# Softmax sums of the dilated attention combined as one number a token, and its value products in plain f32

## The chip, the cores and the metric

The kernel runs as one program on 1 core of one Trainium2 chip. A core has TensorE (PE in the profile, its weight loads are PEld), VectorE (DVE), ScalarE (ACT), GpSimd (POOL) and SyncE (SP), which here only issues DMAs. The metric is device time in microseconds (us), the median of some runs; lower is better.

## The reference

The reference is a decoder trunk of two layers over 1024 tokens of width 1024, all in f32. Layer 0 mixes with latent attention (`mla`) and forgetting attention (`fox`); layer 1 mixes with dilated attention and with sparse attention (compressed `cmp`, selected `sel`, window `win`). Each layer ends with an MLP and a gated embedding. What the change touches is the dilated attention: three groups with distances 1, 4 and 16 between keys, four heads each, whose outputs are merged head by head with the softmax denominators as weights:

```
for g, (w, d) in enumerate(((128, 1), (512, 4), (2048, 16))):
    idx = t[:, None] - offsets[g][None, :]                  # keys t, t-d, t-2d, ..
    logits = einsum(q[g], k[g][idx]) * scale + bias
    lse = logsumexp(logits);  p = exp(logits - lse)
    outs.append(einsum(p, v[g][idx]));  lses.append(lse)
wts = softmax(stack(lses, axis=0), axis=0)                  # over the three groups
return einsum('gbhq,gbqhd->bqhd', wts, stack(outs))
```

So each token has, for each head, three minima, three sums and three weights; each weight multiplies 64 output elements.

## The kernel before

All products that must be exact to f32 are made of float32r operands (TensorE's fast format for 4-byte numbers): an operand is split into a high part and the low rest, and two or three products are added up. A projection streams the weights in units (`RAW`, 512 KB a load), POOL makes `WH` (the high part) and `WL` (the rest) of each (lines 873 and 875), and PE multiplies (line 1035).

The attention of a layer is a list of jobs. A job is one kind and one pair of heads; layer 1 has d1, d4, d16, cmp for pair 0, the same four for pair 1, then sel, win, sel, win. `d1`, `d4`, `d16` are the three distances. A job has 16 tasks: 8 blocks of 128 queries for head e=0, then 8 for head e=1. Two tasks are a chunk, four a half. `build_attention` makes a list of steps, one for a task, and every engine walks the same list in order, each doing its part and waiting on semaphores:

- PE: `logits(t)` (line 1181), then `values` of a chunk that ended 5 steps ago (line 1211), then `turn(t)` of the task two steps back, which transposes the probabilities into one of two `TR` banks (line 1195). At the start of a job `turn_v` transposes the values `RV` into the same two banks (line 1159).
- DVE: scale, bias and row minimum of the logits, into `PBS` and `NML` (line 1785). ACT: exponential and row sum (line 1453).
- ACT copies the transposed probabilities from `TR` to `PT` as the high part (line 1447), and DVE subtracts it from `TR` for the low part (line 1796). The values go the same way into `VS` (lines 1436 and 1767). The products of the high part of one head and of the low part of the other fall on the rows of the other head in the bank `OP`, so ACT copies those rows to `CORR` (line 1421) and DVE adds both.
- Dilated only: DVE adds into `DU` (line 1826). When a half of e=1 ends, POOL spreads the row sums and row minima of both heads over 64 columns each (`SPREAD`, line 941, twice), PE transposes them through the same two `TR` banks (`turn_spread`, line 1224, 8 transposes), ACT copies the sums to `DL` (line 1427) and DVE the minima to `DM` (line 1830). `DL` and `DM` so hold each number 64 times, and have the shape of the outputs.
- `merge`: over the steps after d16, that is inside cmp, DVE takes minima, differences, products, sums and reciprocals of 128x1024 tiles (lines 1853 to 1869), ACT exponentials (line 1459), and POOL weights and adds the outputs (lines 950 to 962).

SP issues the loads of the attention in one queue, in order: per job `RV` (512 KB) and for each head six pieces of `QK` (256 KB each) and a `BIAS`. The buffers of `QK` are one for each e, so a load for the next job waits for the last logits of the same e (`s_qk`), line 707. A cmp job needs no `RV` and only two pieces of `QK` a head.

After the attention, POOL makes `WH` and `WL` of the first unit of the output projection once its last `XL` is written.

Of the kernel before, what the change touches and what calls it, by code (L numbers as in the profile page):

```python
# [21 lines left out]
P = 128  # L22
# [63 lines left out]
MERGE_STEPS = 12  # L86
POOL_STEPS = 7
# [102 lines left out]
MERGE_PIECES = 14  # L190
# [22 lines left out]
class Group:  # L213
# [3 lines left out]
    def __init__(self, seq, first, n, tr, half=None, what=None):  # L217
        self.seq, self.ring, self.first, self.n, self.tr = seq, (seq - 1) % 2, first, n, tr
        self.half, self.what = half, what


class Task:


    def __init__(self, no, job, e, i):
# [4 lines left out]
        self.col = no % 16  # L230
# [34 lines left out]
def build_attention():  # L265
# [3 lines left out]
    n = dict(load=0, bias=[0, 0], head=[0, 0], raw=0, ops=0, mask=0, rl=0, spread=0, dl=0, fin=0, xl=0, cor=0, xo=0)  # L269
    phases = {}  # L270
    for name, plan in (("even", EVEN_JOBS), ("odd", ODD_JOBS)):
        ph = Phase()
        ph.name, ph.jobs, ph.tasks = name, [], []
        for kind, pair in plan:
# [6 lines left out]
            for e in range(2):  # L281
# [15 lines left out]
                for h in range(2):  # L297
# [35 lines left out]
    count = dict(seq=0, a=0)  # L333
    groups = []

    def group(first, size, half=None, what=None):
        count["seq"] += 1
        count["a"] += half is None
        groups.append(Group(count["seq"], first, size, count["a"], half, what))
        return groups[-1]  # L340

    for ph in phases.values():
# [3 lines left out]
        merging, ph.merged = [], {}  # L346
        for s in range(len(ts) + VALUE_LAG + 2 + MERGE_PIECES):
# [10 lines left out]
            st.merge = [(p, s - s0) for p, s0 in merging if 0 < s - s0 <= MERGE_PIECES]  # L358
            if st.out and st.out is st.out.job.halves[-1] and st.out.job.kind == "d16":
                merging.append((st.out.job.pair, s))  # L360
                ph.merged[st.out.job.pair] = st.out.fin
# [6 lines left out]
            if st.start and st.start.kind != "cmp":  # L368
                st.start.vgroups = [group(g, 4) for g in range(2)]
            if st.turn:  # L370
                for g0 in range(0, len(st.turn.blocks), 4):
                    st.turn.groups.append(group(g0, min(4, len(st.turn.blocks) - g0)))
                st.turn.turned = count["a"]
            if st.norm and st.norm.e == 1:
                st.norm.groups = [group(0, 4, st.norm, what)
                                  for what in (("sums", "minima") if st.norm.job.kind in DILATED else ("inverse",))]
# [5 lines left out]
    for ph in phases.values():  # L382
        end = Phase()
        end.tasks, end.chunks, end.halves = ph.tasks[-1].no + 1, ph.jobs[-1].chunks[-1].no + 1, ph.jobs[-1].halves[-1].no + 1
# [3 lines left out]
        end.xl, end.fin = ph.jobs[-1].halves[-1].xl, ph.jobs[-1].halves[-1].fin  # L388
# [10 lines left out]
def program(nc, ins, out):  # L399
# [5 lines left out]
    with ctx:  # L405
# [110 lines left out]
        y_h = dram("y_h", (DC, P, S))  # L516
        b_rows = dram("b_rows", (16, BROW_N))
# [57 lines left out]
        s_o = sem("s_o")  # L575
        s_xo = sem("s_xo")
# [6 lines left out]
        s_dl = sem("s_dl")  # L583
# [12 lines left out]
        s_md = sem("s_md")  # L596
        s_cmp = sem("s_cmp")
# [59 lines left out]
        def group_free(eng, g):  # L657

            if g.seq > 2:
                x = pt_groups[g.seq - 3]  # L660
                if x.what == "sums":
                    eng.wait_ge(s_dl, x.half.dl)
                elif x.half:
                    eng.wait_ge(s_fin, x.half.fin)
                else:
                    eng.wait_ge(s_ptD, x.tr)

# [14 lines left out]
        def _(sp):  # L682
# [1505 lines left out]
```

## Time and profile before

| | us |
|---|---|
| median of 3 runs | 3186.12 (3182.68 to 3191.12) |
| profiled execution, its own time | 3180.44 |
| its span (first to last instruction) | 3178.6 |
| PE busy | 2913.9 (92%) |
| DVE busy | 1241.0 (39%) |
| ACT busy | 898.4 (28%) |
| POOL busy | 947.3 (30%) |
| mean granted TensorE clock | 0.961 of full |

The page also cuts the span in 40 equal slices of 79.5 us. In the slices 24 to 27, about 1830 to 2150 us, the busy share of PE falls to 7 to 8 tenths and the one of DVE rises to 4 to 7 tenths; the granted clock there is 0.7 to 0.9. The dilated and compressed jobs of layer 1 lie there. In nearly all other slices PE is at 9 tenths.

A row of the trace's timeline gives start, duration, engine, line of the kernel, operation, written tile<-read tiles, shape and count of merged instructions, and in brackets the idle time before and what ended it. A DMA row shows how long SP took to issue it.

### The profile page before, as it was taken

What the parts mean: (1) busy time and instruction counts of PE and PEld (TensorE: products, weight loads), DVE (VectorE), ACT (ScalarE), POOL (GpSimd) and SP (SyncE); (2) the same over time, 40 slices, a digit from 0 to 9 for tenths busy, and PEclk for the clock granted to TensorE, in tenths of its full rate; (3) what the DMA queues carried; (4) which work ended last, traced back from release to release, by engine and by line L of the source; (5) the groups of instructions that cost most, each with busy time, mean ns of one, the idle gap of its engine ahead of it and who ended that gap; (6) DMA issues with size and microseconds to landing.
All of it is one profiled execution on the core that took longest, in us unless ns stands there. A gap on an engine that the chain in (4) does not pass through costs nothing.

```text
span 3178.6 us, 37130 instructions
## 1 busy us (share of the span) xinstructions
PE 2913.9 (92%) x13684; PEld 2381.1 (75%) x13684; DVE 1241.0 (39%) x1893; ACT 898.4 (28%) x1613; POOL 947.3 (30%) x622
## 2 busy tenths in 40 slices
PE   8996888889999999999999976867889999999999
PEld 5785777767888888876788865756668888888867
DVE  3425777414222222225423147687252222222254
ACT  3304666423110010025200035656340001011141
POOL 2330144342333333342233202121423333333332
PEclk9998999999999999999999986779999999999999
DMA  4336532110111111111235264444201111111111
GB/s 154 126 116 179 126 82 65 74 47 34 47 53 46 46 46 53 46 53 53 80 130 217 80 162 105 113 113 122 80 33 51 49 46 46 51 48 46 60 40 73
DMA packets 73792, 253.67 MB, mean 80 GB/s; under 512 B 9699, under 2 KB 13283, under 8 KB 73367
## 3 DMA queue, kind: packets, MB, share of 16 engines
q1 hardware_dynamic: 58728, 196.35, 20.4%
q10 hardware_dynamic: 14944, 55.74, 4.5%
q8 instruction: 73, 1.20, 0.2%
q14 instruction: 47, 0.39, 0.0%
HBM read 203.99 MB, written 52.78 MB: 81 GB/s over the span
## 4 chain that ended last, share of the span: by engine, by line
PE 80%; DVE 10%; issue 4%; ACT 2%; DMA 2%; POOL 1%; SPq 0%; DVEq 0%; ACTq 0%; POOLq 0%
PE ACC L1035 67%; PE OP L1211 3%; PE ACC L1181 3%; PE TR L1195 3%; PE OP L1105 2%; DVE PT L1796 1%; DVE XL L1653 1%; DVE H L1673 1%; ACT PT L1447 1%; DVE T L1670 1%; PE TR L1224 1%; DVE PB L1785 1%; DVE XF L1842 1%; PE TR L1159 1%; DVE M L1702 0%
## 5 line engine op out<-in xcount | busy, mean ns | idle before, releaser
L873 POOL CAST WH<-RAW 128x1024 fp32r<-128x1024 f32 x203 | 214.2, 1055 | 1544.8 <-PE ACC L1035 1526.2
L1035 PE MATMUL ACC<-XH,WH 128*128 128x512 f32 x1792 | 575.1, 402 | 54.2 <-DVE XL L1653 26.8
L1035 PE MATMUL ACC<-XL,WH 128*128 128x512 f32 x1792 | 557.1, 392 | 0.0
L1035 PE MATMUL ACC<-XH,WL 128*128 128x512 f32 x1792 | 556.5, 392 | 0.0
L875 POOL TENSOR_TENSOR WL<-RAW,WH 128x1024 fp32r<-128x1024 f32 x203 | 491.1, 2419 | 24.8 <-POOL WH L873 1.5
L1035 PEld LDWEIGHTS ACC<-XH,WH 128*128 128x128 f32 x1792 | 338.1, 190 | 153.5 <-issue 72.6
L1035 PEld LDWEIGHTS ACC<-XL,WH 128*128 128x128 f32 x1792 | 339.6, 189 | 71.9
L1035 PEld LDWEIGHTS ACC<-XH,WL 128*128 128x128 f32 x1792 | 339.3, 189 | 71.9
L1409 ACT ACTIVATE HH<-T 128x1024 fp32r<-128x1024 f32 x64 | 67.9, 1061 | 1149.7 <-DVE T L1695 1149.7
L1702 DVE TENSOR_TENSOR M<-M,ACC 128x1024 f32<-128x1024 f32 x128 | 156.3, 1221 | 482.6 <-PE ACC L1035 480.4
L1035 PE MATMUL ACC<-HH,WH 128*128 128x512 f32 x1024 | 316.7, 390 | 3.3 <-DVE M L1702 3.1
L1035 PE MATMUL ACC<-HL,WH 128*128 128x512 f32 x1024 | 315.3, 389 | 0.0
L1035 PE MATMUL ACC<-HH,WL 128*128 128x512 f32 x1024 | 315.2, 389 | 0.0
L1181 PE MATMUL ACC<-QK 128*128 128x512 f32 (+3 forms) x864 | 234.7, 385 | 12.2 <-DMA QK<-y_odds 5.7
L1695 DVE SCALAR_TENSOR_TENSOR T<-ACC,R 128x1024 f32<-128x1024 f32 x64 | 78.4, 1225 | 418.7 <-PE ACC L1035 418.0
L1796 DVE TENSOR_TENSOR PT<-TR,PT 128x512 fp32r<-128x512 f32 (+4 forms) x416 | 191.4, 477 | 108.6 <-ACT PT L1447 104.1
L1035 PEld LDWEIGHTS ACC<-HH,WH 128*128 128x128 f32 x1024 | 191.0, 188 | 48.2 <-issue 9.5
L1035 PEld LDWEIGHTS ACC<-HL,WH 128*128 128x128 f32 x1024 | 192.2, 188 | 40.1
L1035 PEld LDWEIGHTS ACC<-HH,WL 128*128 128x128 f32 x1024 | 192.2, 188 | 40.0
L1447 ACT ACTIVATE PT<-TR 128x512 fp32r<-128x512 f32 (+4 forms) x416 | 168.7, 427 | 171.7 <-PE TR L1195 167.2
L1195 PE MATMUL TR<-IDENT,PB 128*128 128x128 f32 x840 | 135.9, 283 | 54.0 <-DVE PT L1796 21.7
L1181 PEld LDWEIGHTS ACC<-QK 128*128 128x128 f32 x864 | 164.1, 222 | 24.5 <-issue 6.3
(193 smaller groups left out, 3406.0 us busy)
## 6 DMA issues: line engine op xcount, KB each, us to landing
RAW<-in_w SPq DMA_DIRECT2D x203, 512.0 KB, 3.5
QK<-y_odds SPq DMA_DIRECT2D x128, 256.0 KB, 5.1
y_odds<-HALVES ACTq DMA_DIRECT2D x16, 1024.0 KB, 5.3
QK<-y_foxs SPq DMA_DIRECT2D x48, 256.0 KB, 5.5
y_foxs<-HALVES ACTq DMA_DIRECT2D x8, 1024.0 KB, 5.1
y_kv<-Q ACTq DMA_DIRECT2D x8, 512.0 KB, 2.6
BIAS<-y_f SPq DMA_DIRECT2D x8, 512.0 KB, 7.2
H<-in_xT ACTq DMA_DIRECT2D x8, 512.0 KB, 7.2
```

The costliest lines, as they stand in the source:

```text
L873: nc.gpsimd.tensor_copy(WH[:, slot], RAW[:, slot]).then_inc(s_whi, 1)
L875: nc.gpsimd.tensor_tensor(WL[:, slot], RAW[:, slot], WH[:, slot].bitcast(F32), ALU.subtract).then_inc(s_split, 1)
L1035: mm = nc.tensor.matmul(acc[:, h * HALF:(h + 1) * HALF], w(k), x[:, k, h * HALF:(h + 1) * HALF], start=first and k == k0 and w is ws and x ...
L1105: mm = nc.tensor.matmul(OP[:, h], ONES[:], Q[:, (q + c) % 2, h * HALF:(h + 1) * HALF], start=c == 0, stop=c == n - 1)
L1181: mm = nc.tensor.matmul(score_bank(t, c0, c1), x, k[:, c0:c1], start=m == 0, stop=m == len(passes) - 1 and not masked)
L1195: tr = nc.tensor.transpose(TR[0:w, g.ring, y * P:(y + 1) * P], prob(t)[:, x * w:(x + 1) * w], IDENT[:])
L1211: mm = nc.tensor.matmul(OP[:, c.half.no % 2, col + c0:col + c1], v, pt, start=c.opens and n == 0 and hl == 0, stop=c.closes and n == len(o ...
L1409: nc.scalar.activation(HH[:, t.idx], x, ACT.Square).then_inc(s_hhi, 1)
L1447: nc.scalar.activation(PT[0:r, c.buf, 0, k0:k0 + g.n, m * P:(m + 1) * P], src.rearrange("p (k q) -> p k q", q=P), ACT.Copy).then_inc(s_ptA, 1)
L1695: V_.scalar_tensor_tensor(out=x, in0=ACC[:, t.pair], scalar=0.0, in1=R[:], op0=ALU.max, op1=ALU.mult).then_inc(s_evD, 1)
L1702: V_.tensor_tensor(M[:, t.idx], M[:, t.idx], ACC[:, t.pair], ALU.add).then_inc(s_evD, 1)
L1796: V_.tensor_tensor(lo, TR[0:r, g.ring, 0:g.n * P].rearrange("p (k q) -> p k q", q=P), hi.bitcast(F32), ALU.subtract).then_inc(s_ptD, 1)
```

## The change

**Dilated value products in plain f32.** For d1, d4 and d16 the transposed values and probabilities are copied once, by DVE, to f32 tiles `VF` and `PF`; ACT's high copies, DVE's low rests, `CORR` and the sum of both are gone. One plain f32 product for each key block, of the values of both heads, takes the place of two float32r products. Of its result ACT copies the rows of the head to `DU`.

**Combination on one number a token.** `SPREAD`, `turn_spread`, `DL` and `DM` are gone for dilated jobs. `NML` gets 32 columns. After each dilated job, SP writes its row minima and sums from `NML` to DRAM in the order of the tokens (`sums_out`, 4 DMAs: sums or minima, head). After d16 it loads all of them as a tile `ZS` of 128x96 (a partition holds 8 tokens), DVE and ACT compute the three weights in 8 and 1 small instructions, SP writes them to DRAM and loads them back broadcast over 64 partitions each (`weights_in`, 6 loads `DW` of 256 KB). POOL multiplies the outputs with them in halves of 512 columns, 15 steps after d16's last logits or later.

**Weights of the output projection.** In both layers POOL makes `WH` and `WL` of the first two units at the fifth task from the end of the attention, instead of after it.

The core of the diff:

```diff
+            def sums_out(j):
+                g = DILATED.index(j.kind)
+                sp.wait_ge(s_exp, j.tasks[-1].no + 1)
+                for m in range(2):
+                    for e in range(2):
+                        c0 = j.tasks[NB * e].col
+                        src, dst = NML[:, m, c0:c0 + NB], z_sums[j.pair, g, m, e]
+                        if j.kind == "d1":
+                            dst = dst.rearrange("(i p) -> p i", p=P)
+                        elif j.kind == "d4":
+                            src = src.rearrange("p (b a) -> p b a", b=2)
+                            dst = dst.rearrange("(b p a) -> p b a", b=2, a=4)
+                        else:
+                            dst = dst.rearrange("(p i) -> p i", i=NB)
+                        sp.dma_start(dst, src, allow_slow_non_contiguous=j.kind == "d1").then_inc(s_zs[g], 16)
+            def weights_in(j):
+                p = j.pair
+                for g in range(3):
+                    sp.wait_ge(s_zs[g], 16 * 4 * (p + 1))
+                sp.dma_start(ZS[:], z_sums[p].rearrange("g m e (p i) -> p (g m e) i", i=NB)).then_inc(s_zr, 16)
+                sp.wait_ge(s_md, MERGE_STEPS * (p + 1))
+                sp.dma_start(z_weights[p].rearrange("g e (p i) -> p (g e) i", i=NB), ZW[:]).then_inc(s_zw, 16)
+                sp.wait_ge(s_zw, 16 * (p + 1))
+                wait(sp, s_ox, 2 * p)
+                for g in range(3):
+                    for e in range(2):
+                        load(DW[rows_of_head(e), g], z_weights[p, g, e:e + 1].to_broadcast([HD, S]), s_dw)
...
# SP, at the end of a job's loads
+                if before and before.kind in DILATED:
+                    sums_out(before)
+                    if before.kind == "d16":
+                        weights_in(before)
...
# POOL, attention
+                    if st.logits is ph.tasks[-5]:
+                        weights(out, units_of=slice(0, 2))
...
# PE, values
+                    if j.kind in DILATED:
+                        for n, (k, c0, c1) in enumerate(order):
+                            mm = nc.tensor.matmul(OP[:, c.half.no % 2, col + c0:col + c1], VF[:, j.slot, k],
+                                                  PF[:, c.buf, k - c.k0, c0:c1], start=c.opens and n == 0,
+                                                  stop=c.closes and n == len(order) - 1, skip_group_check=True)
+                        mm.then_inc(s_pv, 1)
+                        return
...
# ACT, correction
+                    if h.job.kind in DILATED:
+                        if h.job.kind == "d1" and h is h.job.halves[0]:
+                            wait(act, s_ox, 2 * h.job.pair)
+                        dst, src = by_token(h, DU[rows, DILATED.index(h.job.kind)], OP[rows, h.no % 2])
+                        nc.scalar.activation(dst, src, ACT.Copy).then_inc(s_ow, 1)
+                        return
...
# DVE, low_turned (low_v has the same for VF)
+                        if t.kind in DILATED:
+                            dve.wait_ge(s_tr, g.tr)
+                            wait(dve, s_pv, c.no - 1)
+                            V_.tensor_copy(PF[:, c.buf, k0:k0 + g.n, m * P:(m + 1) * P],
+                                           TR[:, g.ring, 0:g.n * P].rearrange("p (k q) -> p k q", q=P)).then_inc(s_ptD, 1)
+                            continue
...
# DVE, scores: the columns of NML are used again two jobs later
+                    if t.first_of_head and t.e == 0 and t.job.no > 1 and t.job.before.before.kind in DILATED:
+                        j = t.job.before.before
+                        dve.wait_ge(s_zs[DILATED.index(j.kind)], 16 * 4 * (j.pair + 1))
...
# DVE, merge (the 12 steps on 128x1024 tiles are gone)
+                    if k == 7:
+                        dve.wait_ge(s_zr, 16 * (j.pair + 1))
+                        step(1, V_.tensor_tensor(ZM[:], ZS[:, 0, 0], ZS[:, 1, 0], ALU.min))
+                        step(2, V_.tensor_tensor(ZM[:], ZM[:], ZS[:, 2, 0], ALU.min))
+                        step(3, V_.tensor_tensor(ZD[:], ZS[:, :, 0], each(ZM), ALU.subtract))
+                    elif k == 9:
+                        dve.wait_ge(s_mg, j.pair + 1)
+                        step(4, V_.tensor_tensor(ZW[:], ZD[:], ZS[:, :, 1], ALU.mult))
+                        step(5, V_.tensor_tensor(ZL[:], ZW[:, 0], ZW[:, 1], ALU.add))
+                        step(6, V_.tensor_tensor(ZL[:], ZL[:], ZW[:, 2], ALU.add))
+                        step(7, V_.reciprocal(ZL[:], ZL[:]))
+                        step(8, V_.tensor_tensor(ZW[:], ZD[:], each(ZL), ALU.mult))
```

What moves is seen in the order of the instructions. On SP, behind the loads of job d4, pair 0 (`s_qk`, `s_ttr`, `s_tr`, `s_exp` are what a row waits for: logits, scores, transposes, exponentials), before:

```order
L707 DMA QK<-y_odds 64x1024 x5
L707 DMA BIAS<-b_d 128x256 [waits s_ttr]
L707 DMA RV<-y_odd 128x1024 [waits s_tr]
L707 DMA QK<-y_odds 64x1024 [waits s_qk]
L707 DMA QK<-y_odds 64x1024 x5
```

and now:

```order
L725 DMA QK<-y_odds 64x1024 x5
L725 DMA BIAS<-b_d 128x256 [waits s_ttr]
L743 DMA z_sums<-NML 128x8x1 [waits s_exp]
L743 DMA z_sums<-NML 128x8x1 x3
L725 DMA RV<-y_odd 128x1024 [waits s_tr]
L725 DMA QK<-y_odds 64x1024 [waits s_qk]
L725 DMA QK<-y_odds 64x1024 x5
```

Four writes of d1's sums stand ahead of the loads for d16. On SP behind the loads of cmp, pair 0 (the last two `QK` rows are the queries of e=1), before:

```order
L707 DMA QK<-y_odds 64x1024 [waits s_qk]
L707 DMA QK<-y_odds 64x1024
L707 DMA RV<-y_odd 128x1024 [waits s_tr]
L707 DMA QK<-y_odds 64x1024 [waits s_qk]
L707 DMA QK<-y_odds 64x1024 x5
L707 DMA BIAS<-b_d 128x256 [waits s_ttr]
```

and now:

```order
L725 DMA QK<-y_odds 64x1024 [waits s_qk]
L725 DMA QK<-y_odds 64x1024
L743 DMA z_sums<-NML 128x8 [waits s_exp]
L743 DMA z_sums<-NML 128x8 x3
L751 DMA ZS<-z_sums 128x12x8 [waits s_zs2,s_zs1,s_zs0]
L753 DMA z_weights<-ZW 128x6x8 [waits s_md]
L725 DMA DW<-z_weights 64x1024 [waits s_zw]
L725 DMA DW<-z_weights 64x1024 x5
L725 DMA RV<-y_odd 128x1024 [waits s_tr]
L725 DMA QK<-y_odds 64x1024 [waits s_qk]
L725 DMA QK<-y_odds 64x1024 x5
```

The load for the next d1 stands behind four DMA steps, each of which waits for the one before or for DVE. On DVE inside cmp, pair 0 (the `ISA` rows are the scores of a task, `PT` its low rest), before and now:

```order
L1785 ISA PBS,NML<-ACC,CMPMASK 128x64 [waits s_tr,s_qk]
L1785 ISA NML 128x1
L1853 TENSOR_TENSOR DMIN<-DM_92,DM_93 128x1024 [waits s_fin]
L1796 TENSOR_TENSOR PT<-TR,PT 64x128 [waits s_ptA]
L1785 ISA PBS,NML<-ACC,CMPMASK 128x64 [waits s_tr,s_qk]
L1785 ISA NML 128x1
L1856 TENSOR_TENSOR DMIN<-DMIN,DM_94 128x1024 [waits s_md]
L1796 TENSOR_TENSOR PT<-TR,PT 64x128 [waits s_ptA]
```

```order
L1863 ISA NML 128x1
L1931 TENSOR_TENSOR ZM<-ZS 128x16 [waits s_zr]
L1932 TENSOR_TENSOR ZM<-ZM,ZS 128x16 [waits s_md]
L1933 TENSOR_TENSOR ZD<-ZS,ZM 128x48 [waits s_md]
L1880 TENSOR_TENSOR PT<-TR,PT 64x128 [waits s_ptA,s_md]
L1863 ISA PBS,NML<-ACC,CMPMASK 128x64 [waits s_tr,s_qk]
```

One 128x1024 instruction between two tasks, twelve times over, has become three and five tiny ones at two places, the first of which waits for a DMA (`s_zr`).

## Rows read from the trace of the kernel before

**Rows 1.** Stretches of layer 1, cut at each job's first logits; columns as first row.

```profile
core 0: us, PE busy (x) PEld busy (x) DVE busy (x) ACT busy (x) POOL busy (x), PEclk, DMA share, GB/s
1890.98:1914.20 23.22, 19.80 (x122) 17.40 (x121) 16.41 (x56) 16.88 (x56) 2.41 (x4) 1.00 0.69 162
1914.20:1937.24 23.04, 18.92 (x100) 17.63 (x99) 14.96 (x53) 14.94 (x51) 2.35 (x4) 0.71 0.38 83
1937.24:1976.23 38.99, 21.11 (x95) 17.49 (x96) 33.05 (x75) 19.09 (x63) 14.98 (x8) 0.54 0.46 110
1976.23:2003.85 27.62, 19.73 (x111) 16.46 (x109) 22.31 (x60) 16.51 (x54) 8.70 (x7) 0.72 0.44 102
2050.09:2089.46 39.37, 22.23 (x95) 18.53 (x95) 32.99 (x75) 19.08 (x63) 14.97 (x8) 0.50 0.48 118
2089.46:2111.18 21.72, 15.64 (x67) 11.54 (x66) 18.41 (x34) 9.95 (x25) 7.58 (x5) 0.65 0.21 54
2111.18:2128.96 17.78, 14.06 (x104) 12.38 (x102) 14.76 (x38) 14.16 (x33) 0.61 (x1) 1.00 0.53 130
```

**Rows 2.** Groups by line and form, 1873.25 to 2128.96 us: busy us, mean ns | idle before.

```profile
L1826 DVE TENSOR_TENSOR DU<-OP,CORR 64x512 f32<-64x512 f32 x24 | 23.2, 966 | 5.1 <-ACT CORR L1421 4.7
L1224 PE MATMUL TR<-IDENT,SPREAD 128*128 128x128 f32 x112 | 23.0, 351 | 2.7 <-DVE VS L1767 1.3 <-DVE PT L1796 1.1
...
L1869 DVE RECIPROCAL DL<-DL 128x512 f32<-128x512 f32 x4 | 13.4, 3347 | 0.0
...
L1830 DVE COPY DM<-TR 128x512 f32<-128x512 f32 x12 | 11.3, 944 | 0.4
```

**Rows 3.** Waits of PE, 1872 to 2112 us: total us, times, longest.

```profile
PE TR L1195 <- DVE PT L1796: 38.4, 31, 4.2
```

**Rows 4.** Timeline of PE: line 1105 is plain f32, line 1211 float32r.

```profile
49.69 1.88 PE L1105 MATMUL OP<-Q,ONES 128*128 128x512 f32 x4
...
1882.44 0.80 PE L1211 MATMUL OP<-PT,VS 128*128 128x256 f32 x6
```

**Rows 5.** Timeline of SP: start, time to issue.

```profile
1887.81 3.98 SPq L707 DMA_DIRECT2D QK<-y_odds  x6
...
1951.14 3.66 SPq L707 DMA_DIRECT2D QK<-y_odds  x6
```

**Rows 6.** Stretches of 1 to 8 us; the last two columns are DMA share and GB/s.

```profile
1952.00:1959.00 7.00, 4.42 (x18) 3.25 (x17) 6.97 (x17) 4.48 (x12) 2.55 (x1) 0.50 0.96 221
1959.00:1960.00 1.00, 0.00 (x0) 0.00 (x0) 1.00 (x4) 0.34 (x2) 1.00 (x2) 0.50 0.77 157
1960.00:1968.00 8.00, 2.09 (x10) 1.69 (x10) 8.00 (x13) 3.13 (x12) 4.28 (x2) 0.50 0.00 0
1892.00:1898.00 6.00, 5.00 (x32) 4.21 (x31) 4.19 (x13) 3.58 (x12) 1.23 (x2) 1.00 1.03 239
1898.00:1899.00 1.00, 1.00 (x10) 1.00 (x10) 0.79 (x5) 0.82 (x3) 0.00 (x0) 1.00 0.28 98
```

**Rows 7.** Small DMAs at the program's start: when SP issued them.

```profile
2.54 0.49 SPq L686 DMA_DIRECT2D IDENT<-in_ident  x1
3.07 0.50 SPq L686 DMA_DIRECT2D QKVG<-in_qkvg  x1
```

**Rows 8.** DMA issues, 0 to 30 us: KB, us from issue to landing.

```profile
IDENT<-in_ident SPq DMA_DIRECT2D x1, 64.0 KB, 10.1
...
QKVG<-in_qkvg SPq DMA_DIRECT2D x1, 1.5 KB, 10.9
```

**Rows 9.** Timeline at the ends of both attentions; brackets: idle before, releaser.

```profile
607.22 1.19 PE L1035 MATMUL ACC<-XH,WH 128*128 128x512 f32 x2 [7.40 <-POOL WL L875]
...
2238.85 0.61 POOL L941 COPY SPREAD<-RL 128x512 f32<-128x512 f32 x1 [15.12 <-DVE RL L1814]
...
2257.13 1.04 POOL L873 CAST WH<-RAW 128x1024 fp32r<-128x1024 f32 x1
...
2260.94 1.19 PE L1035 MATMUL ACC<-XH,WH 128*128 128x512 f32 x2 [10.24 <-POOL WL L875]
```

More of the change, by code:

```diff
@@ L213, with __init__ @@
 class Group:
-    def __init__(self, seq, first, n, tr, half=None, what=None):
+    def __init__(self, seq, first, n, tr, high, half=None):
         self.seq, self.ring, self.first, self.n, self.tr = seq, (seq - 1) % 2, first, n, tr
-        self.half, self.what = half, what
+        self.half, self.high = half, high
 class Task:
@@ L331, in build_attention, with group @@
             t.pb_free = -1
-    count = dict(seq=0, a=0)
+    count = dict(seq=0, a=0, high=0)
     groups = []
-    def group(first, size, half=None, what=None):
+    def group(first, size, half=None, whole=False):
         count["seq"] += 1
         count["a"] += half is None
-        groups.append(Group(count["seq"], first, size, count["a"], half, what))
+        count["high"] += half is None and not whole
+        groups.append(Group(count["seq"], first, size, count["a"], count["high"], half))
         return groups[-1]
@@ L357, in build_attention @@
             st.out = ph.steps[-1].norm if ph.steps else None
[L358 to L361, printed above, removed]
+            st.merge = [(j, s - s0) for j, s0 in merging if 0 < s - s0 <= MERGE_PIECES]
+            if st.logits and st.logits is st.logits.job.tasks[-1] and st.logits.kind == "d16":
+                merging.append((st.logits.job, s))
             st.split = None
@@ L368, in build_attention @@
             if st.start and st.start.kind != "cmp":
-                st.start.vgroups = [group(g, 4) for g in range(2)]
+                st.start.vgroups = [group(g, 4, whole=st.start.kind in DILATED) for g in range(2)]
             if st.turn:
                 for g0 in range(0, len(st.turn.blocks), 4):
-                    st.turn.groups.append(group(g0, min(4, len(st.turn.blocks) - g0)))
+                    st.turn.groups.append(group(g0, min(4, len(st.turn.blocks) - g0), whole=st.turn.kind in DILATED))
                 st.turn.turned = count["a"]
-            if st.norm and st.norm.e == 1:
-                st.norm.groups = [group(0, 4, st.norm, what)
-                                  for what in (("sums", "minima") if st.norm.job.kind in DILATED else ("inverse",))]
+            if st.norm and st.norm.e == 1 and st.norm.job.kind not in DILATED:
+                st.norm.groups = [group(0, 4, st.norm)]
             ph.steps.append(st)
@@ L387, in build_attention @@
             j.free = jobs[j.no - 2].chunks[-1].no + 1 if j.no > 1 else 0
-        end.xl, end.fin = ph.jobs[-1].halves[-1].xl, ph.jobs[-1].halves[-1].fin
+        last = ph.jobs[-1].halves[-1]
+        end.xl, end.fin, end.cor, end.whole = last.xl, last.fin, last.cor, last.whole
         ph.end = end
@@ L516, in program @@
         y_h = dram("y_h", (DC, P, S))
+        z_sums = dram("z_sums", (2, 3, 2, 2, S))
+        z_weights = dram("z_weights", (2, 3, 2, S))
         b_rows = dram("b_rows", (16, BROW_N))
@@ L596, in program @@
         s_md = sem("s_md")
+        s_zs = [sem(f"s_zs{g}") for g in range(3)]
+        s_zr = sem("s_zr")
+        s_zw = sem("s_zw")
+        s_dw = sem("s_dw")
         s_cmp = sem("s_cmp")
@@ L660, in group_free @@
                 x = pt_groups[g.seq - 3]
-                if x.what == "sums":
-                    eng.wait_ge(s_dl, x.half.dl)
-                elif x.half:
+                if x.half:
                     eng.wait_ge(s_fin, x.half.fin)
@@ L666, in group_free, with taken @@
                     eng.wait_ge(s_ptD, x.tr)
+        def taken(eng, h):
+            if h and h.job.kind in DILATED:
+                eng.wait_ge(s_ow, h.whole)
+            elif h:
+                eng.wait_ge(s_o, h.cor)
         def run(eng, n, body):
```

232 lines of the change are left out of this document (108 added, 124 removed).

## The prediction, made before the changed kernel ran

> **What bounds the kernel now.** I read the 40 slices first: PE is the bound nearly everywhere, and the change touches none of that. Only the dilated and compressed jobs of layer 1 fall out. So the second view is the busy time of each engine between the first logits of one job and of the next [rows 1]. The reader is to see two kinds of stretch. In cmp (39.0 us for 16 small tasks) DVE is busy 33.1 us and PE 21.1 us at half clock: the twelve wide instructions of the merge stand between the tasks. They spill over into the next job, which takes 27.6 us after pair 0 and 21.7 us for a half of sel after pair 1, where the half behind it, without a merge, takes 17.8. In d4 and d16 (23.2 and 23.0 us) PE is busy 19 to 20 us, and stops for the two `TR` banks. The waits of PE say the same: 38.4 us of it for DVE's `PT` [rows 3]. By lines [rows 2], DVE spends 23.2 us on `DU`, 11.3 us on the copies of the minima, 13.4 us on four reciprocals, and PE 23.0 us of overlapped time on 112 spread transposes, 96 of them for dilated jobs.
>
> The third view is the DMA queue, which the engines' rows don't show. A set of six `QK` pieces and the `BIAS` is issued at 1951.14 us [rows 5], its packets fill the DMA engines for 7.0 * 0.96 + 0.77 = 7.5 us, at 221 GB/s, and end at 1959.8 us [rows 6]: 8.7 us from the issue. The set for a head may be issued only when the eighth logits of that head's buffer in the job before are done, and is needed eight tasks later. So no half of a dilated job can be shorter than 8.7 us once the queue is fed like this, and a job not shorter than 17.5 us. Before, this floor is hidden by the 23 us of a job: the last set for d4 is issued at 1887.81 us [rows 5] and the queue is empty at 1898.3 [rows 6], while d4 goes on to 1914.20 [rows 1].
>
> **What is removed.** DVE loses `DU`, the minima and the merge, some 80 us over both pairs; ACT loses the high copies; PE 96 transposes, at some 0.11 us 10 us, and the stalls around them. What I estimate for compute alone of d4 or d16 is about 17 to 18 us, and of cmp about 16 tasks of 1 us. Both are at or under what the DMAs now allow, so the DMAs decide.
>
> **Value products.** Six float32r products take 0.80 us, so about 0.11 us each; four instructions of plain f32 with 512 columns take 1.88 us, about 0.43 us each [rows 4], and a product is two such instructions. By columns, a product of 256 costs 2 * 0.21 = 0.43 us against 2 * 0.11 before. With 128 columns I take 2 * 0.11, no more than before, as the weight load sets it. There are 8 wide key blocks a head (4 in d1, 4 in d4), 4 heads: 32 * 0.2 = 6.4 us more, up to 12.8 at half clock. It roughly cancels the transposes that go. It lies in jobs that are at the load's floor, so I cost it at nothing; without that cover it costs these 6.4 to 12.8 us.
>
> **What is added to the queue.** The rows of the order on SP give the pieces: d1's sums are 4 DMAs of 128x8x1, that is 4096 packets of one number; d4's 1024 of 16 bytes, d16's 512 of 32 bytes; `ZS` is 1536 and `z_weights` 768 of 32 bytes. On each of 16 engines this is 256, 64, 32, 96 and 48 packets a pair. No row shows such packets alone. The nearest: `IDENT` and `QKVG`, of 128 rows each, were issued at 2.54 and 3.07 us [rows 7] and landed 10.1 and 10.9 us later [rows 8], so at 12.64 and 13.97. The 128 packets of 12 bytes took at most 1.33 us, 8 on each engine: 166 ns a packet. Much of that can be the turns of the other queue, which loaded x at the same time, so the lower end is next to nothing. I take 40 ns, a quarter of the upper end, and keep 0 and 166 for the range. So d1's sums take 10.2 us of the queue, d16's 1.3, `ZS` 3.8, `z_weights` 1.9.
>
> **Now job by job, against [rows 1].**
> - d1 of pair 0: none. The queue is full of its own and d4's loads until 1898.3 us [rows 6], and d4 can't start earlier.
> - d4: 7.3 us until the queue is empty, then d1's sums 10.2, `RV` 2.2, the set for d16 7.5, 0.3 to land: 27.5 us against 23.2. **+4.3.** In pair 1 the same: **+4.3.**
> - d16: two sets of 8.8, 17.6 us against 23.0: **-5.4** in each pair. d4's sums (2.6 us) go out beside it.
> - cmp of pair 0. Count from its first logits. d16's sums are issued from 1.2 us, four in 2 us, and land at 6. `ZS` has 0.4 to issue, 1.5 to start and land, 3.8 of packets: 12. DVE waits for it at the seventh task, which it would reach at about 7 us; behind this wait on DVE stand the low rests and the scores, so ACT and PE stop within two tasks: 5 us of stall, where the merge had its own. Three small instructions, two tasks, five small ones: 16.5. `z_weights` lands at 20.8. `DW`, 1.57 MB at 230 GB/s, 6.8 us and 1.4 to start: 29.0. Only behind it come `RV` (2.3) and the set for d1 (7.5): 38.8 against 39.0. **-0.2.** Compute alone would have been done at some 21. What DVE gives free, SP's queue takes: the set that was issued at 1951.14, inside cmp [rows 5], now waits for three DMA round trips.
> - d1 of pair 1: at the floor, 18.0 with the first tasks at half clock, against 27.6: **-9.6.**
> - cmp of pair 1: the same chain to 29.0, then `RV` 2.3, `QK` 6.9, `BIAS` (512 KB) 2.3: 40.5 against 39.4. **+1.1.**
> - first half of sel: as its second, 17.8 against 21.7. **-3.9.**
> - POOL's merge (6 products, 4 sums, 4 others, all of half size) needs some 18 us after `DW`, beside the next job; ACT's first `DU` of d1 in pair 1 waits for it and comes at about the same time. I cost it at 0; 2 us if it is late.
> - the ends: PE waits for `WH` and `WL`, which POOL begins at 2257.13 us, 3.8 us before PE's first product at 2260.94; at the other end PE waits for `WL` too [rows 9]. POOL idled 15.1 us before its row at 2238.85, so the same work fits there. PE then follows the last `XL`: 3.4 us each, **-6.8.**
>
> Sum: 4.3 + 4.3 - 5.4 - 5.4 - 0.2 - 9.6 + 1.1 - 3.9 - 6.8 = -21.6. The profiled execution took 3180.4 us, so it would be 3158.8. The median of the runs is 5.7 us above it, 3186.1, and gives 3164.5; I say **3164**.
>
> On the path lie 256 + 32 + 96 + 48 = 432 packets an engine and pair, so each ns of the packet time moves the result by 0.86 us.
>
> The Trainium skill bears on this. Its page "DMA: Bandwidth & Descriptors", section "Rules for kernel authors", says that a strided last dimension becomes one descriptor per element; section "Bandwidth" has a floor of about 10.5 ns a packet over all engines, which would be 43 us for d1's 4096 numbers; and "Specifications" adds that below 512 B the DMA does a read-modify-write. By that rule the kernel would be slower, some 110 us above my sum. The upper end that I read from the start-up rows is nearly the same number, but no run here shows the packets without a second queue beside them.
>
> **Rivals.**
> 1. *Small packets are dear, and the kernel gets slower.* At 166 ns d1's sums hold the queue for 42.5 us. d16's loads stand behind them, d16 starts 32 us later than I say, in both pairs, and the three later transfers take 29 us a pair where I took 7. Time: 3164.5 + 126 * 0.864 = 3273. It decides from 65 ns on (no gain at all), and is slower by over 0.3% from 76 ns: at 90 ns 3208. For it: [rows 7, 8] and one number per packet, written to DRAM, which no row has. Against: those rows were read beside a full queue.
> 2. *Small packets are nearly free.* Then d4 falls to its floor and the chain in cmp shortens by 7 us: 3164.5 - 34.6 = 3130, and some less if PE keeps full clock in d16 (0.71 now [rows 1]). For it: nothing in the queue is long in bytes.
> 3. *Plain f32 becomes the bound.* If PE and not the loads sets the dilated jobs, the 6.4 to 12.8 us of products come back: 3171 to 3177. For: PE is at 19.8 of 23.2 us in d4 [rows 1]. Against: it waits at the banks for DVE, and these waits go.
> 4. *Nothing to measure.* The chain of the sums gives back what the small tasks gain, 3186, at 55 to 75 ns.
>
> **How the numbers follow.** What can be told from no change is 0.3%, 9.6 us. The forecast (20 to 54 ns a packet, 3147 to 3177) has 0.40, with rival 3 inside it at 0.05 more; rival 2 0.21; rival 4 0.12; rival 1 0.22. So faster 0.66, same 0.12, slower 0.22. The range reaches from rival 2 with some clock gained, 3125, to 93 ns a packet, 3210; the forecast's own is 3147 to 3177.
>
> **What would show it.** The `z_sums` writes of d1 should land 10 us after their start, and d16's first logits come about 27.5 us after d4's. DVE should wait for `ZS` some 5 us in each cmp, and PE for a `QK` load 15 us or more at the starts of d1 in pair 1 and of sel. The jobs d16 should take 17.6 us. PE's wait for POOL's `WL` at both ends should be gone. I am wrong if d4 shrinks (the packets are cheap), if PE waits at the banks in the dilated jobs as before, or if cmp ends early.

## The result, and the profile after

The changed kernel took **3162.26 us** (median of 4 runs, 3160.58 to 3164.19), the kernel before beside it 3184.4 (4 runs, 3182.23 to 3191.12): a ratio of **0.9927, 95% interval 0.9913 to 0.9941**. The kernel is faster by 22 us, clear of the noise though under 1%, and 2 us from the predicted 3164. The sum came out; several of its terms did not, and their errors cancelled.

The profiled run of after took 3164.19 us, its highest, and the one of before 3180.44, below its four timed runs. The two traces so differ by 16 us where the medians differ by 22. First the page's engines and its chain:

```profile
PE 2896.8 (92%) x13588; PEld 2372.0 (75%) x13588; DVE 1163.2 (37%) x1849; ACT 858.4 (27%) x1489; POOL 923.8 (29%) x610
...
PE 81%; DVE 8%; DMA 4%; issue 3%; ACT 2%; SPq 1%; POOL 1%; DVEq 0%; ACTq 0%; POOLq 0%
```

DVE lost 78 us of work, and the path's share of DMA is 4% (2% before). The same stretches as in [rows 1], cut at each job's first logits (the last column but one is the DMA share):

```profile
1886.46:1922.59 36.13, 20.50 (x104) 18.67 (x104) 12.07 (x51) 11.53 (x36) 0.00 (x0) 0.81 0.88 113
1922.59:1937.65 15.06, 14.75 (x81) 14.29 (x82) 8.29 (x45) 10.83 (x34) 0.00 (x0) 0.88 0.61 124
1937.65:1969.45 31.80, 14.99 (x81) 12.44 (x80) 11.84 (x70) 13.25 (x54) 6.80 (x6) 0.59 0.69 153
1969.45:1993.62 24.17, 21.39 (x108) 18.91 (x109) 14.86 (x55) 11.79 (x38) 10.52 (x10) 0.69 0.65 147
1993.62:2030.92 37.30, 19.16 (x106) 17.85 (x105) 12.62 (x52) 11.54 (x36) 0.00 (x0) 0.79 1.02 120
...
2045.85:2076.96 31.11, 14.99 (x80) 12.42 (x80) 11.83 (x70) 14.44 (x56) 6.80 (x6) 0.61 0.70 154
2076.96:2093.81 16.85, 14.66 (x67) 11.69 (x67) 12.04 (x31) 9.71 (x25) 10.56 (x10) 0.71 0.70 163
```

d4 has become 13 and 14 us longer (36.1 and 37.3, before 23.2 twice), everything else shorter. The DMA share of d4 is 0.88 and 1.02, while it moves only 113 and 120 GB/s. Inside the first d4 stretch, in pieces:

```profile
1887.00:1894.00 7.00, 7.00 (x42) 6.74 (x42) 3.89 (x18) 3.92 (x13) 0.00 (x0) 1.00 1.07 201
1894.00:1903.00 9.00, 6.24 (x34) 5.54 (x32) 3.42 (x18) 4.14 (x15) 0.00 (x0) 0.96 0.63 2
1903.00:1912.00 9.00, 4.75 (x23) 4.24 (x21) 3.04 (x13) 3.48 (x11) 0.00 (x0) 0.85 0.86 47
1912.00:1919.00 7.00, 1.97 (x8) 1.57 (x8) 1.38 (x2) 0.00 (x0) 0.00 (x0) 0.54 0.94 189
```

The loads are through at 1894. For 9 us next to nothing moves (2 GB/s): these are d1's sums. In the next 9 us 47 GB/s make some 420 KB, and all of d1's sums are 16 KB, so what moves there is `RV`, at about a fifth of the rate of the first row. By the semaphore events of the trace the last of d1's sums lands at 1913.0 us and `RV` at 1915.1; only then do the `QK` for d16 run at the full rate. The waits of 1865 to 2110 us (total, times, longest) name the same releasers:

```profile
PE TR L1221 <- DMA RV<-y_odd: 28.1, 3, 12.2
PE ACC L1243 <- DMA QK<-y_odds: 27.9, 7, 6.0
...
PE TR L1257 <- DVE PT L1880: 5.6, 10, 1.1
...
DVE ZM L1931 <- DMA ZS<-z_sums: 2.3, 2, 1.2
```

Where PE waited for DVE at the `TR` banks [rows 3], it now waits 56 us for loads (19 us in the same window before). In cmp the sums' chain of transfers on SP:

```profile
1938.97 2.01 SPq L743 DMA_DIRECT2D z_sums<-NML  x4
1943.20 0.37 SPq L751 DMA_DIRECT2D ZS<-z_sums  x1
1948.21 0.37 SPq L753 DMA_DIRECT2D z_weights<-ZW  x1
1950.21 3.70 SPq L725 DMA_DIRECT2D DW<-z_weights  x6
1953.95 0.59 SPq L725 DMA_DIRECT2D RV<-y_odd  x1
1954.90 4.27 SPq L725 DMA_DIRECT2D QK<-y_odds  x6
```

with, from issue to landing (KB, median us):

```profile
ZS<-z_sums SPq DMA_DIRECT2D x2, 48.0 KB, 2.5
...
z_weights<-ZW SPq DMA_DIRECT2D x2, 24.0 KB, 2.0
```

`DW` is issued 12.6 us after cmp's first logits (1937.65); d1 begins 19.2 us later. Finally the end of the second attention, which answers to [rows 9]: the last `XL`, and PE behind it.

```profile
2241.37 1.26 POOL L981 TENSOR_TENSOR XL<-XF,XH 128x512 fp32r<-128x512 f32 x1
...
2243.05 1.20 PE L1097 MATMUL ACC<-XH,WH 128*128 128x512 f32 x2 [6.93 <-issue]
```

### The profile page after: what moved, and what is told of

Same layout as the page of the kernel before. It is cut to its first block, busy times and chain, and to the rows that moved or that the text cites. A ratio compares the mean times of both kernels' runs of the same rounds, so it can differ in the third digit from the quotient of the medians.

```text
span 3162.4 us, 36743 instructions
## 1 busy us (share of the span) xinstructions
PE 2896.8 (92%) x13588; PEld 2372.0 (75%) x13588; DVE 1163.2 (37%) x1849; ACT 858.4 (27%) x1489; POOL 923.8 (29%) x610
## 2 busy tenths in 40 slices
DMA packets 91069, 257.03 MB, mean 81 GB/s; under 512 B 26211, under 2 KB 29795, under 8 KB 90647
## 4 chain that ended last, share of the span: by engine, by line
PE 81%; DVE 8%; DMA 4%; issue 3%; ACT 2%; SPq 1%; POOL 1%; DVEq 0%; ACTq 0%; POOLq 0%
PE ACC L1097 68%; PE ACC L1243 4%; PE OP L1280 3%; PE TR L1257 3%; DMA QK<-y_odds 2%; PE OP L1167 2%; DVE XL L1723 1%; DVE PT L1880 1%; DVE H L1743 1%; DVE T L1740 1%; SPq L725 1%; ACT PT L1517 1%; DVE PB L1863 1%; PE OP L1270 1%; DVE XF L1914 1%
## 5 line engine op out<-in xcount | busy, mean ns | idle before, releaser
L1243 PE MATMUL ACC<-QK 128*128 128x512 f32 (+3 forms) x864 | 235.1, 387 | 34.9 <-DMA QK<-y_odds 27.9
L1880 DVE TENSOR_TENSOR PT<-TR,PT 128x512 fp32r<-128x512 f32 (+2 forms) x320 | 158.3, 517 | 97.4 <-ACT PT L1517 94.3
L1257 PE MATMUL TR<-IDENT,PB 128*128 128x128 f32 x840 | 137.4, 286 | 51.9 <-DVE PT L1880 19.2
L1517 ACT ACTIVATE PT<-TR 128x512 fp32r<-128x512 f32 (+2 forms) x320 | 137.7, 458 | 154.4 <-PE TR L1257 151.2
```

Source lines behind the costliest of these rows:

```text
L1243: mm = nc.tensor.matmul(score_bank(t, c0, c1), x, k[:, c0:c1], start=m == 0, stop=m == len(passes) - 1 and not masked)
L1257: tr = nc.tensor.transpose(TR[0:w, g.ring, y * P:(y + 1) * P], prob(t)[:, x * w:(x + 1) * w], IDENT[:])
L1517: nc.scalar.activation(PT[0:r, c.buf, 0, k0:k0 + g.n, m * P:(m + 1) * P], src.rearrange("p (k q) -> p k q", q=P), ACT.Copy).then_inc(s_ptA, 1)
L1880: V_.tensor_tensor(lo, TR[0:r, g.ring, 0:g.n * P].rearrange("p (k q) -> p k q", q=P), hi.bitcast(F32), ALU.subtract).then_inc(s_ptD, 1)
```

## The experiments

All were timed beside the kernel before, which took 3184.1 to 3186.4 in these comparisons. "After" is the changed kernel, 3162.3. The table gives the stretches that the verdicts use, in us (d4 of pair 0 / d4 of pair 1, and so on), from each profiled run.

| kernel | median | ratio to before, 95% | d4 | d16 | cmp | d1 of pair 1 |
|---|---|---|---|---|---|---|
| before | 3184.4 | 1 | 23.2 / 23.2 | 23.0 / 23.0 | 39.0 / 39.4 | 27.6 |
| after | 3162.3 | 0.9927 (0.9913 to 0.9941) | 36.1 / 37.3 | 15.1 / 14.9 | 31.8 / 31.1 | 24.2 |
| A: d1's sums in rows of 32 bytes | 3129.1 | 0.982 (0.9802 to 0.9837) | 18.5 / 18.7 | 14.6 / 17.9 | 31.8 / 33.4 | 22.6 |
| B: d1's sums written twice | 3186.1 | 1.0001 (0.9992 to 1.0011) | 48.7 / 49.5 | 14.6 / 15.0 | 31.5 / 31.0 | 22.6 |
| C: before, with early `WH`, `WL` | 3179.4 | 0.9975 (0.9964 to 0.9987) | | | | |
| D: after, value products as before | 3171.3 | 0.9957 (0.994 to 0.9973) | 31.5 / 35.6 | 18.5 / 19.1 | 32.1 / 32.8 | 24.6 |
| E: d1's and d4's sums from ACT's queue | 3160.3 | 0.9931 (0.9911 to 0.9952) | 33.2 / 31.8 | 14.5 / 17.3 | 32.2 / 31.2 | 24.2 |
| F: loads ahead of the weights | 3139.6 | 0.9859 (0.9839 to 0.9879) | 34.5 / 35.7 | 15.4 / 15.1 | 18.1 / 19.3 | 26.9 |
| G: E and F | 3134.9 | 0.9846 (0.983 to 0.9863) | 32.1 / 35.8 | 15.1 / 16.9 | 18.0 / 19.3 | 27.9 |
| H: d1's sums turned on PE | 3127.4 | 0.9819 (0.9801 to 0.9837) | 18.6 / 18.9 | 14.8 / 18.0 | 29.9 / 32.6 | 24.2 |
| I: F and H | 3110.0 | 0.9761 (0.9741 to 0.9781) | 18.5 / 18.6 | 17.5 / 16.0 | 18.1 / 18.7 | 27.3 |
| J: I, `DW` behind the second head's loads | 3108.0 | 0.9755 (0.9739 to 0.9771) | 18.6 / 19.6 | 16.7 / 16.0 | 18.1 / 18.6 | 23.2 |

**A. d1's sums in rows of 32 bytes** (its output differs: the sums of d1 land in another order of tokens).

```diff
-    if j.kind == "d1":
-        dst = dst.rearrange("(i p) -> p i", p=P)
-    elif j.kind == "d4":
+    if j.kind == "d4":
         src = src.rearrange("p (b a) -> p b a", b=2)
```

> The changed kernel, but d1's sums and minima go to DRAM in rows of 8 numbers (32 bytes, 128 packets a DMA instead of 1024 of 4 bytes). The tokens of d1's weights are then in a wrong order, so the output differs. Theory (the number of packets costs): the stretch from d4's first logits to d16's, 36.1 and 37.3 us in the changed kernel, falls to about 19 in both pairs; total 3162 - 34 = 3128. Rival (four more DMAs in the queue cost, whatever their packets): the stretch stays over 33 us, total 3155 to 3165.

Same bytes, same place in the queue, an eighth of the packets: 3129.1, and both d4 stretches fall to the loads' floor. The first:

```profile
1891.29:1909.80 18.51, 18.31 (x104) 17.30 (x104) 11.12 (x50) 11.48 (x36) 0.00 (x0) 1.00 0.90 203
```

What lengthened d4 is that d1's sums go out in 4-byte packets. The bytes and the place in the queue are the same in A, but number and size of the packets change together, so A doesn't tell which of the two is paid for.

**B. The same 4 writes issued a second time**, to a tensor that nobody reads.

```diff
+    if j.kind == "d1":
+        for m in range(2):
+            for e in range(2):
+                sp.dma_start(z_again[...].rearrange("(i p) -> p i", p=P), NML[:, m, c0:c0 + NB], ..)
```

> The changed kernel, with d1's four writes of single numbers issued a second time, to a DRAM tensor that nobody reads. Theory (packets of 4 bytes fill the queue, some 70 ns each on an engine, 256 on each engine): another 18 us a pair in the stretch of d4, total 3162 + 36 = 3198. Rival (a fixed cost of about 2 us for the lot, or a latency that overlaps): 3164 to 3168.

```profile
1886.67:1935.32 48.65, 19.16 (x104) 17.87 (x104) 12.09 (x51) 11.39 (x36) 0.00 (x0) 0.72 1.11 83
```

3186.1: the second lot cost 23.8 us, 12 a pair, where the first costs 16.6 a pair (after less A). The sign is as expected, the size two thirds of it. By the stretches of pair 0, 256 packets an engine took 17.6 us the first time (36.1 less 18.5) and 12.5 the second, 69 and 49 ns each. In D the whole d4 stretch was 31.5, which makes 51. The price isn't one number. Part of the difference is seen in B's trace, cut where the rate changes:

```profile
1894.00:1916.00 22.00, 9.86 (x54) 9.19 (x54) 6.77 (x32) 7.63 (x24) 0.00 (x0) 0.82 1.25 2
1916.00:1927.00 11.00, 0.00 (x0) 0.00 (x0) 0.00 (x0) 0.00 (x0) 0.00 (x0) 0.50 0.95 55
1927.00:1935.30 8.30, 1.97 (x8) 1.59 (x9) 1.38 (x2) 0.00 (x0) 0.00 (x0) 0.50 1.00 228
```

In after the stretch at 2 GB/s lasts 9 us and the slow one behind it 12 us (1903 to 1915, at 61 GB/s). The second lot adds 13 us to the first of these and nothing to the other: with one lot or with two, the loads behind the last small packets start slowly once. Why they do, and why D's d4 is shorter than after's, was not found.

**C. The kernel before, with `WH` and `WL` of the output projections made early.**

```diff
+                    if st.logits is ph.tasks[-5]:
+                        weights(out, units_of=slice(0, 2))
```

> The kernel before with one part of the change alone: WH and WL of the first two units of both output projections are made at the fifth task from the end of the attention. Theory: PE's wait for WL at both ends goes, 3.4 us each, total 3184.4 - 6.8 = 3177.6. Rival (XL is written last anyway and something else holds PE, or POOL is late elsewhere): 3182 to 3186.

3179.4, 7.0 us below before (by the interval 4 to 11): the ends were worth what the sum said, 6.8.

**D. The combination alone**: after, but probabilities and values of dilated jobs again in high and low parts, with `CORR` and the addition on DVE.

```diff
-                            V_.tensor_copy(PF[...], TR[...]).then_inc(s_ptD, 1)
+                        V_.tensor_tensor(lo, TR[...], hi.bitcast(F32), ALU.subtract).then_inc(s_ptD, 1)
```

> The changed kernel with the value products of dilated jobs as before (high and low parts in float32r, CORR and the sum on DVE), so the combination on one number a token and the early weights alone. Theory (d4 is held by the load queue, so only d16 and d1 feel the value products): d4's stretch stays at 36 to 37 us, d16's goes from 15 to 18 or 19, total 3162 + 8 to 14 = 3173. Rival (the plain f32 products bring most of the gain): 3180 or more. Second rival (they bring nothing, their longer PE time is paid back): 3162 or less.

3171.3 against after's 3162.3: plain f32 brought 9 us by the medians. The two intervals just meet (0.9941 and 0.994), so its size is rough; D's profiled run was its fastest, 3165.6, and is only 1.4 us above after's. Its d4 stretches are shorter than after's (31.5 and 35.6 us), where I had expected 36 to 37; that looks like the same unsteady price. Its products over d4 and d16 of pair 0 (busy us, mean ns) in after and in D:

```profile
L1270 PE MATMUL OP<-PF,VF 128*128 128x128 f32 x49 | 9.0, 291 | 0.0
L1270 PE MATMUL OP<-PF,VF 128*128 128x256 f32 x22 | 8.1, 455 | 0.0
```

```profile
L1271 PE MATMUL OP<-PT,VS 128*128 128x128 f32 x50 | 10.2, 324 | 0.0
L1271 PE MATMUL OP<-PT,VS 128*128 128x256 f32 x22 | 5.3, 327 | 0.0
```

They cost PE more (17.1 for 15.5 us), all of it in the 256 columns. The gain is seen in d16 (7.6 us over both pairs), which D takes through in 18.5 and 19.1 us, at a low granted clock:

```profile
1917.81:1936.27 18.46, 16.47 (x81) 15.86 (x82) 11.27 (x49) 11.90 (x48) 0.00 (x0) 0.59 0.49 103
2028.46:2047.60 19.14, 17.47 (x82) 16.82 (x82) 11.29 (x49) 12.02 (x48) 0.00 (x0) 0.50 0.45 94
```

After has 81 PE instructions there too, but 8.3 us of DVE for 11.3, 34 instructions on ACT for 48, and a granted clock of 0.88. Of the 3.4 us by which its first d16 is shorter than D's, 1.7 are in PE's busy time (14.8 for 16.5, at the higher clock) and 1.7 in its stops.

**E. The sums of d1 and d4 issued from ACT's queue**, one of the four DMAs at a time between the tasks of the next job.

```diff
+                    if t and t.kind in ("d4", "d16"):
+                        place = t.no - t.job.tasks[0].no
+                        if place % 3 == 1 and place < 12:
+                            sums_piece(t.job.before, place // 3)      # act.dma_start(..)
```

> The changed kernel, with the sums of d1 and d4 issued from ACT's queue, one DMA at tasks 1, 4, 7 and 10 of the next job; same packets, same bytes. Theory (d16's loads wait because they stand behind the small packets in SP's queue; between two queues the engines take turns): d4's stretch falls from 36 to about 20 us, total 3162 - 32 = 3130, with ACT losing 2 us in places. Rival (the small packets hold the engines themselves, from whatever queue): the stretch stays at 33 us or more, total 3155 or more.

My theory here was that the loads only stand *behind* the packets in SP's queue. It fell: 3160.3, no different from after. The loads now overtake on SP (`RV` for d16 is issued at 1894.43 us), yet they are slow all the same, and PE waits 13.4 us for that `RV`:

```profile
1890.00:1900.00 10.00, 9.79 (x57) 9.11 (x55) 5.92 (x24) 5.07 (x18) 0.00 (x0) 1.00 1.23 194
1900.00:1910.00 10.00, 4.68 (x18) 4.26 (x18) 2.34 (x11) 3.31 (x9) 0.00 (x0) 0.69 0.92 72
...
PE TR L1221 <- DMA RV<-y_odd: 13.4, 1, 13.4
```

Small packets hold up the loads whichever queue they come by. What they fill, the DMA engines or something ahead of them that both queues share, isn't shown: in after the engines' share is 0.63 in the 9 us in which only 2 GB/s move. The Trainium skill's page "DMA: Bandwidth & Descriptors", section "Issuing engines are not separate DMA queues", says that DMAs of all issuers run on the same 16 engines and interleave; this run agrees with it.

**F. The first loads of the next job ahead of the weights.** In cmp SP issues `RV`, `QK` and `BIAS` of the next job's first head before it waits for the weights; products with `DW` start 4 tasks later, and pair 1 has its own `DU` tiles.

```diff
-                            weights_in(before)
+                            zs_in(before)
...
+                        if e == 0 and before and before.kind == "cmp":
+                            weights_in(before.before)
```

> The changed kernel, with SP's order changed behind cmp: ZS, then RV, QK and BIAS of e=0 of the next job, and only then the weights out and DW in. The merge on POOL starts 19 steps after d16 instead of 15, and pair 1 has a second set of DU tiles, so that ACT need not wait for the merge. Theory (cmp's 31.8 and 31.1 us are its own 17 and the loads that stand behind DW): cmp's stretches fall to about 20 each, total 3162 - 22 = 3140, the d4 stretches stay at 36. Rival (the loads are limited by bytes, DW included): cmp falls by 3 us at most, or what it gains comes back in d1 of pair 1: 3155 or more.

3139.6, as expected, and cmp falls from 31.8 and 31.1 us to 18.1 and 19.3. In its first cmp the loads stand in the gap in which DVE makes the weights:

```profile
1939.70 0.37 SPq L751 DMA_DIRECT2D ZS<-z_sums  x1
1940.11 0.70 SPq L726 DMA_DIRECT2D RV<-y_odd  x1
1940.86 3.67 SPq L726 DMA_DIRECT2D QK<-y_odds  x6
...
1945.51 0.37 SPq L756 DMA_DIRECT2D z_weights<-ZW  x1
1952.45 3.65 SPq L726 DMA_DIRECT2D DW<-z_weights  x6
```

So cmp's 31 us in after are the order of the queue. The price shows two rows on: `z_weights`, of 24 KB, now lands behind 2 MB of loads, 6.9 us after its issue where it took 2.0, and the second head's `QK` stands behind that wait. d1 of pair 1 is 2.7 us longer.

**G. E and F together.**

> Both together: sums of d1 and d4 from ACT's queue, and the next job's loads ahead of the weights. Theory: the two gains add up, 3162 - 32 - 22 = 3108, below the kernel before by 2.4%. Rival (once the queue is free, TensorE's products or the loads of the dilated jobs bind): 3120 to 3130.

3134.9, short of my 3108 and of the rival's 3120 to 3130: F's gain is there, E's isn't, as E alone had shown. The 4.7 us below F lie within the two intervals.

**H. d1's sums turned on PE**: the reference's output, and rows of 512 bytes.

```diff
+    for m in range(2):                     # behind the last turn of a d1 job
+        tr = nc.tensor.transpose(TR[0:16, g.ring, m * P:(m + 1) * P], NML[:, m, c0:c0 + 16], IDENT[:])
+    V_.tensor_copy(ZT[:], TR[0:16, g.ring, 0:2 * P])
+    sp.dma_start(z_sums[j.pair, 0].rearrange("m e (i p) -> (e i) m p", p=P), ZT[:])
```

> The changed kernel, with the sums of the d1 jobs brought into token order on TensorE (two transposes of 128x16 behind the job's last turn, one VectorE copy of 16x256) and written as 32 rows of 512 bytes in one DMA, in place of 4096 elements of 4 bytes in four. The output is the same. My theory (the d4 stretch is long by the 4-byte packets alone): as with d1's sums in rows of 32 bytes, 33 us below the changed kernel, 3129, and the d4 stretches at 18 to 19 us; the transposes and the copy cost under 1 us a pair. Rival: the step through the shared transpose ring and VectorE holds up the first turns of d4, 2 us a pair or more, 3134 or over.

3127.4, in line with A. What takes the place of 18 us of packets:

```profile
1890.08 0.38 PE L1270 MATMUL TR<-IDENT,NML 128*16 128x128 f32 x2
...
1890.74 0.40 DVE L1971 COPY ZT<-TR 16x256 f32<-16x256 f32 x1
...
1891.17 0.34 SPq L736 DMA_DIRECT2D z_sums<-ZT  x1
```

**I. F and H.**

> Both remedies together: d1's sums turned on TensorE and written as 32 rows, and the next job's loads ahead of the weights in the queue in cmp (the merge four steps later, a second set of buffers for the outputs of pair 1). The output is the same. My theory: the two act in different stretches (d4, and cmp), so they add: 3139.6 less 33 = 3106. Rival: the stretches share a cushion of early loads, so that a stretch freed hands its wait to the next one, and a third or more of the second gain is lost: 3115 or over.

3110.0: of the 33 us that H should add to F, 29.6 came, and 3106 lies inside I's interval. The two lie in different stretches, and little is handed on. d4 is at 18.5 and cmp at 18.1 at once:

```profile
1892.26:1910.78 18.52, 18.32 (x106) 17.41 (x106) 11.28 (x51) 11.54 (x36) 0.00 (x0) 1.00 0.87 197
1928.26:1946.40 18.14, 14.63 (x81) 12.47 (x80) 10.98 (x69) 13.25 (x53) 0.61 (x1) 0.67 0.73 158
```

**J. I, with `DW` fetched behind the second head's loads.**

```diff
-                        if e == 0 and before and before.kind == "cmp":
-                            weights_in(before.before)
+                        if before and before.kind == "cmp":
+                            (dw_in if e else weights_in)(before.before)
```

> As the kernel with both remedies (3110), but in cmp SyncE waits for the weights of the tokens (z_weights) and fetches DW only behind the loads of the second head of the next job; the products with DW start two steps later. The output is the same. My theory: what was left of the wait for loads in d1 of pair 1 (PE waited 3.7 us for the second head's QK, whose issue stood behind SyncE's wait for z_weights from 1939.7 to 1946.3) goes, and nothing else: d1 of pair 1 falls from 27.3 to 23.6 us and the time by 3.7, to 3106. Rival: the load of the second head is then held by the channels, not by the queue (RV of the next job and DW share them), or the products with DW end late and hold the next users of POOL: 3109 to 3112.

```profile
1934.80 0.43 SPq L762 DMA_DIRECT2D z_weights<-ZW  x1
1939.52 4.39 SPq L729 DMA_DIRECT2D QK<-y_odds  x6
...
1944.58 3.65 SPq L729 DMA_DIRECT2D DW<-z_weights  x6
```

The second head's `QK` goes out 4.7 us after `z_weights` (10.9 in I, at 1939.30 and 1950.18), and d1 of pair 1 falls from 27.3 to 23.2 us, as expected. The time is 3108.0, and the intervals of I and J overlap: the stretch gained 4 us, the kernel 2 by the medians. Inconclusive; the two jobs behind cmp of pair 1, sel and win, are 0.7 and 0.8 us longer in J's profile, and d4 of pair 1 is 1.0 longer, which may be chance. J and I are the best versions here, 2.4% below before.

## Why the prediction was right, step by step

The time came out as said, the way to it only in part. That d4 would grow by the 4-byte packets, that the order of SP's queue and not compute would set cmp, and that d16, d1 and sel would shrink was right; the sizes were not, and one of the signs that I had named for being wrong, that cmp ends early, came true.

- **d4, +4.3 each, measured +12.9 and +14.1.** The order of transfers was right piece by piece: queue empty 7.5 us after d4's first logits (7.3 expected), first logits of d16 10 us behind the sums (9.7 with 0.3 to land), though most of `RV` had by then moved slowly beside the last of them. Mis-sized was d1's sums, 10.2 us taken and 19 found (1893.9 to 1913.0), or some 70 ns a packet for 40. That lies above the forecast's 20 to 54 ns, in the range of rival 4 (55 to 75).
- **One price for all small packets.** This is the step that failed. 32-byte packets are far cheaper: `ZS` has 1536 of them and landed 2.5 us after its issue, `z_weights` 768 in 2.0. I had taken 5.7 and 4.3 (packets, start and landing). Rival 2 was right for these, and for the 4-byte ones the price of rival 4, or of the forecast's upper end where a lot follows another (49 ns in B).
- **cmp, -0.2 and +1.1, measured -7.2 and -8.3.** `ZS` is issued at 5.6 us (6 expected) but has landed at 8, not 12, so DVE waits 1.2 us for it and not 5. The small instructions are done at 10.6 (16.5), `DW` goes out at 12.6 (20.8). Behind it my 18.0 us stood up: 19.2. PE's waits for loads ahead of d1 of pair 1 are 8.6 us for `RV` and 4.8 for `QK`, 13.4 for the 15 or more that I had named. That SP's queue and not compute sets cmp was right, and F shows it.
- **d16, -5.4 each, measured -8.0 and -8.1.** I counted two floors of 8.8 us. The floor is a set that must land before a half can start; behind d16's second half comes cmp, which needs two pieces of `QK`, long there. So that half runs as PE can, in 7 us.
- **d1 of pair 1, -9.6, measured -3.5.** I gave it the loads' floor of 18.0. PE was busy 21.4 of its 24.2 us at a granted clock of 0.69, and J has 23.2 there with the loads on time. The lower level of the clock (1.2 GHz, shown as 0.50 in cmp and through the first half of d1) bounds its first half: 11.2 of 11.9 us busy at 0.52. That it is rival 3, the plain f32 products, isn't shown: D, which has none, takes 24.6 us there.
- **First half of sel, -3.9, measured -4.9; the ends, -6.8, C measured -7.0.** In the trace PE's first product at the second end is 0.4 us behind the last `XL` (3.8 before), and from the last but one spread transpose to it there are 13.0 us where there were 16.4.
- **Value products at nothing.** They gained about 9 us (D), of which 7.6 are seen in d16, along with shorter work on DVE and ACT and a higher clock there. My range of 0 to 12.8 us was all cost; the gain side was missing.
- **Together.** The steps as measured: 12.9 + 14.1 - 8.0 - 8.1 - 7.2 - 8.3 - 3.5 - 4.9 - 7.0 = -20.0, for -21.6 predicted and -22.1 between the medians. The two profiled runs as a whole differ by only 16.2, so this sum closes to some 4 us and no better. The 4-byte packets were 18.4 us worse than said, cmp 16.4 and d16 5.3 better, d1 of pair 1 6.1 worse: the total was right partly by luck. The price of a small packet was the open number, and the range rested on it; with one price for 4 and 32 bytes no value would have given both stretches.

Of the rules weighed, "one descriptor per element" ("Rules for kernel authors", the same page of the Trainium skill) holds: the changed kernel has 26,211 packets under 512 B for 9,699, and by shapes d1's sums are 8,192 of the 16,512 more. The same page's floor of about 10.5 ns a packet ("Bandwidth", measured on loads that GpSimd issues) does not carry over to these DMAs of SP: 4096 packets took 19 us, where an estimate by it gives 43, and the 1536 of `ZS` 2.5 us with start and landing, where it gives 16.

## What to carry to other kernels

Count the packets of a DMA and what is in each: 16 KB written one number at a time held up the loads behind them for 17 to 19 us, and the bytes said nothing of it. Turn such a tile on TensorE first (0.4 us of PE and 0.4 us of DVE here), rather than give it to another queue. When DVE or ACT is relieved by way of DRAM, write down everything that the issuing queue holds behind each new wait, and put the next job's loads into the gaps of the round trip: that order, with a second set of `DU` tiles, was worth 23 us here.

## What the runs showed of the hardware

- 4-byte packets from SBUF to DRAM cost 49 to 73 ns each on an engine (12.5 to 18.8 us for 256), and not the same from run to run; a part of it is a stretch of 11 to 12 us behind the last of them, once for one lot or two, in which the loads move at 55 to 61 GB/s; 32-byte packets cost so little that 96 an engine, read from DRAM, landed within 2.5 us, and 48, written to it, within 2.0, start included. What sets the price between 4 and 32 bytes was not measured apart from the number of packets.
- Two queues do not add up: with the small writes on ACT's queue the loads of SP were slowed instead of held (72 GB/s over 10 us), for the same end.
- A DMA of 24 KB issued behind 2 MB of loads in one queue landed after 6.9 us, alone after 2.0.
- d16 kept PE busy for 16.5 us at a granted clock of 0.59 and 17.5 at 0.50 in D, and 14.8 at 0.88 in after. Fewer stops for DVE and ACT went with the higher clock; which came first can't be read from it.
